# Gate and up weights of an expert as one 2 MB transfer, in a two-layer decoder trunk with 64 experts

## The chip, the cores and the metric

The kernel runs on one core of one Trainium2 chip. The metric is the device time of one execution in microseconds. The changed kernel is timed against the kernel before it on the same chip.

## What is computed

The reference is a decoder trunk of two layers on 256 tokens of width 1024, all in float32. Each layer runs an attention mixer beside a cross-attention into memory tokens, one output projection and a LayerNorm, then a mixture of experts and a second LayerNorm. The part that matters here is the mixture:

```python
def moe_ffn(x, w_router, router_bias, w_gate, w_up, w_down, ws_gate, ws_up, ws_down):
    ...
    gates = jnp.take_along_axis(aff, eidx, axis=-1)
    gates = gates / jnp.sum(gates, axis=-1, keepdims=True) * ROUTED_SCALE
    ...
    def expert_block(args):
        rows, e = args
        xb = x_pad[rows]
        h = jax.nn.silu(xb @ w_gate[e]) * (xb @ w_up[e])
        return h @ w_down[e]
    ...
    routed = jax.ops.segment_sum(yb * row_g[:, None].astype(yb.dtype), row_t, num_segments=n + 1)[:n]
    shared = (jax.nn.silu(xt @ ws_gate) * (xt @ ws_up)) @ ws_down
    return (routed + shared).reshape(B, S, D)
```

There are 64 experts with hidden width 256. Each token goes to 8 of them. `w_gate[e]` and `w_up[e]` are 1024 x 256 and `w_down[e]` is 256 x 1024, so each of the three matrices is 1 MB, and each layer has 192 MB of them.

## The kernel before

Each layer has an attention part and an expert part. The expert part goes through all 64 experts in 32 pairs; this text numbers the pairs of a layer 0 to 31. For each pair TensorE does a **gate pass** (32 matmuls, line 1219), an **up pass** (32 matmuls, line 1238) and a **down pass** (32 matmuls, line 1272). The down pass of a pair comes after the up pass of the next one, so the order on TensorE is gate 1, up 1, down 0, gate 2, up 2, down 1, and so on (function `unit`, line 1317). Between an up pass and the next down pass stand the scatter of an older pair's result (line 1280) and two small transposes (line 1191 and 1245), and in every fourth pair also the gather of the next eight experts' tokens (line 772). At the very end the order is gate 31, scatter, down 30, up 31.

The weights pass through a **ring** of four slots in on-chip memory, one expert (3 MB) in each, so two pairs have room. A slot has three parts of 1 MB: gate, up and down. SyncE (SP in the profile) issues all these transfers, in the order of its program. Each transfer is one instruction on SP at line 433, in `expert`. It moves 128 rows of 8 KB, one to each partition. All three parts are reloaded apart: `reload_gate` (line 455) waits until the gate pass that read the part is done and issues two gate transfers; `reload_up` (line 464) waits until the up pass is done and issues two up transfers; `reload_down` (line 435) waits for the down pass and issues two down transfers. The part of pair j is refilled with the weights of pair j+2. `reload` (line 473) is the first two of these in a row:

```python
reload_gate(l, units, i, b, kept)
reload_up(l, units, i, b, kept)
```

TensorE's gate pass waits for both gate transfers of its pair (semaphores `gate_landed`), its up pass for both up transfers (`up_landed`), its down pass for both down transfers (`down_landed`).

Some pairs are loaded in other ways. Pairs 0 and 1 come in during the attention part, each part apart. Pair 2 has its own lines ahead of the loops (reload_gate at line 578, one expert's up at 580), because one of its up matrices was loaded earlier. Pair 16 is the kept pair: its gate and up matrices, and in layer 0 one down matrix and in layer 1 both, are loaded long before into buffers that are free (`keep`, line 498), so 3 or 4 MB more room is there in the middle of the layer, and the ring need not bring them. Pair 31 is loaded by separate calls at the end of the layer (lines 608 to 610), and its down matrices in halves of 512 KB with rows of 2 KB (`last_down`, line 444). A branch for further rounds (line 614) is not entered with these inputs.

Of the kernel before, what the change touches and what calls it, by code (L numbers as in the profile page):

```python
# [16 lines left out]
P = 128  # L17
# [4 lines left out]
DEPTH = 2  # L22
# [4 lines left out]
NE = 64  # L27
# [48 lines left out]
def build_trunk(nc, x_in, mem_in, w_in_a, sinks, w_in_b, lambda_qk, subln_g, w_mem_kv, w_out, ln_g, ln_b,  # L76
                w_router, router_bias, w_gate, w_up, w_down, ws_gate, ws_up, ws_down, out):
    slopes = [alibi_slopes(MIX_HEADS), alibi_slopes(DIFF_HEADS)]
# [65 lines left out]
    with ExitStack() as ctx:  # L144
# [156 lines left out]
        def expert_loads(s, g, u, dn):  # L301
            n = KT * HID
            return [(s[:, 0:n].rearrange("p (k n) -> p k n", k=KT), by_row_run(g)),
                    (s[:, n:2 * n].rearrange("p (k n) -> p k n", k=KT), by_row_run(u)),
                    (s[:, 2 * n:3 * n].rearrange("p (f n) -> p f n", f=FT), by_row_pair(dn))]
# [102 lines left out]
        def _(sp):  # L408
# [18 lines left out]
            def expert(l, i, k, part):  # L427

                slot = (expert_slot0[l] + k) % RING
                e = RING * i + k  # L430
                srcs = [w[l, bass.ds(e, 1)].rearrange("a r n -> (a r) n") for w in (w_gate, w_up, w_down)]
                dst, src = expert_loads(ring[:, slot, :], *srcs)[part]
                sp.dma_start(dst, src).then_inc(sem(("gate_landed", "up_landed", "down_landed")[part] + f"{k}_{l}"), 16)
# [39 lines left out]
            def reload(l, units, i, b, kept=False):  # L473

                reload_gate(l, units, i, b, kept)
                reload_up(l, units, i, b, kept)

# [17 lines left out]
            def load_up_apart(l):  # L495
                sp.dma_start(up_apart, by_row_run(w_up[l, 0])).then_inc(sem(f"up_apart_{l}"), 16)

            def keep(l, part, e):

                w = (w_gate, w_up, w_down)[part][l, 2 * RES_PAIR + e]  # L500
                sp.dma_start(resident_view(part, e), by_row_pair(w) if part == 2 else by_row_run(w)).then_inc(sem(f"kept_{part}{e}_{l}"), 16)

# [1505 lines left out]
_INS = ["x", "mem", "w_in_a", "sinks", "w_in_b", "lambda_qk", "subln_g", "w_mem_kv", "w_out", "ln_g", "ln_b", "w_router",  # L2008
        "router_bias", "w_gate", "w_up", "w_down", "w_shared_gate", "w_shared_up", "w_shared_down"]

# [15 lines left out]
```

## Time and profile before

| what | value |
|---|---|
| median of 3 runs | 1208.66 us |
| lowest, highest | 1208.44 us, 1208.84 us |
| span of the profiled execution, first to last instruction | 1205.3 us |
| own time of the profiled execution | not given; the median is 3.4 us above its span |
| TensorE busy | 1158.6 us (96%) |
| VectorE, ScalarE, GpSimd busy | 347.2, 301.5, 54.9 us |
| bytes moved, mean rate | 446.93 MB, 371 GB/s |
| packets of SP's queue | 72208 |
| mean granted TensorE clock | 0.996 |
| first gate pass, last up pass, layer 0 | 140.4 us, 576.9 us |
| first gate pass, last up pass, layer 1 | 747.2 us, 1181.8 us |

All times in views of the trace are counted from the first instruction. A transfer is shown by the time at which SP issued it; when it had landed is shown as the time from issue to landing, for a group of transfers as minimum, median and maximum. A view of the chain of work shows, in order of time, the pieces that the end of the program followed from; a piece of DMA in it begins at the issue and ends at the landing.

### The profile page before, as it was taken

What the parts mean: (1) busy time and instruction counts of PE and PEld (TensorE: products, weight loads), DVE (VectorE), ACT (ScalarE), POOL (GpSimd) and SP (SyncE); (2) the same over time, 40 slices, a digit from 0 to 9 for tenths busy, and PEclk for the clock granted to TensorE, in tenths of its full rate; (3) what the DMA queues carried; (4) which work ended last, traced back from release to release, by engine and by line L of the source; (5) the groups of instructions that cost most, each with busy time, mean ns of one, the idle gap of its engine ahead of it and who ended that gap; (6) DMA issues with size and microseconds to landing.
All of it is one profiled execution on the core that took longest, in us unless ns stands there. A gap on an engine that the chain in (4) does not pass through costs nothing.

```text
span 1205.3 us, 22675 instructions
## 1 busy us (share of the span) xinstructions
PE 1158.6 (96%) x8948; PEld 708.5 (59%) x8948; DVE 347.2 (29%) x904; ACT 301.5 (25%) x713; POOL 54.9 (5%) x90
## 2 busy tenths in 40 slices
PE   9999999999999999998999999999999899999985
PEld 6875755555555555554687648555555555555552
DVE  1435512222122212221514456221222222222214
ACT  1453312222121212121213433122221212122212
POOL 1341000000001000000011000000000010000000
PEclk9999999999999999999999999999999999999998
DMA  9944899999999999999990568999999999999995
GB/s 362 364 175 145 310 411 420 422 421 422 422 421 420 410 421 420 422 421 421 387 360 20 205 244 332 411 418 421 422 422 422 422 415 399 409 421 422 421 420 209
DMA packets 74504, 446.93 MB, mean 371 GB/s; under 512 B 6977, under 2 KB 12481, under 8 KB 24897
## 3 DMA queue, kind: packets, MB, share of 16 engines
q1 hardware_dynamic: 72208, 441.22, 89.6%
q10 hardware_dynamic: 2224, 4.72, 1.0%
q8 instruction: 50, 0.82, 0.3%
q14 instruction: 22, 0.17, 0.0%
HBM read 444.86 MB, written 1.05 MB: 370 GB/s over the span
## 4 chain that ended last, share of the span: by engine, by line
PE 76%; DMA 19%; DVE 3%; issue 1%; ACT 1%; SPq 0%; DVEq 0%; ACTq 0%
DMA ring<-in_w_up 19%; PE bank L1238 16%; PE bank L1219 14%; PE bank L1272 13%; PE bank L791 7%; PE bank L772 7%; PE bank L1280 4%; PE bank L830 4%; PE bank L1245 1%; PE bank L1095 1%; PE bank L806 1%; PE bank L1118 1%; PE bank L994 1%; PE bank L1005 1%; DMA ring<-in_w_in_a 1%
## 5 line engine op out<-in xcount | busy, mean ns | idle before, releaser
L1238 PE MATMUL bank<-ring,work 128*64 128x256 f32 x1952 | 225.4, 380 | 13.7 <-DMA ring<-in_w_up 13.7
L1219 PE MATMUL bank<-ring,work 128*64 128x256 f32 x1984 | 227.8, 382 | 8.9 <-DMA ring<-in_w_gate 8.7
L1272 PE MATMUL bank<-ring,work 128*32 128x512 f32 x1904 | 222.0, 595 | 0.2
L1219 PEld LDWEIGHTS bank<-ring,work 128*64 128x64 f32 x1984 | 141.3, 137 | 116.9 <-issue 58.1
L1238 PEld LDWEIGHTS bank<-ring,work 128*64 128x64 f32 x1952 | 147.5, 137 | 81.6 <-issue 20.7
L1942 DVE SCALAR_TENSOR_TENSOR yhalf<-bank,gcol,yhalf 128x512 fp32r<-128x512 f32 x124 | 93.1, 751 | 214.6 <-ACT yhalf L1565 214.6
L1934 DVE TENSOR_TENSOR work<-work,bank 128x256 f32<-128x256 f32 x64 | 27.0, 421 | 367.0 <-PE bank L1238 367.0
L1565 ACT ACTIVATE yhalf<-bank,gcol 128x512 fp32r<-128x512 f32 x124 | 85.2, 687 | 181.4 <-PE bank L1272 181.4
L1272 PEld LDWEIGHTS bank<-ring,work 128*32 128x32 f32 x1904 | 57.4, 109 | 116.9 <-issue 109.9
L1402 ACT ACTIVATE work<-bank 128x512 f32<-128x512 f32 (+4 forms) x177 | 77.9, 440 | 95.1 <-PE bank L772 46.6
L1402 ACT ACTIVATE back<-bank 128x128 fp32r<-128x128 bf16 x64 | 17.7, 277 | 280.2 <-PE bank L1191 280.2
L791 PE MATMUL bank<-xT,ring 128*128 128x256 f32 x352 | 77.7, 379 | 0.0
L772 PE MATMUL bank<-hot,xhalf 128*128 128x256 f32 x512 | 72.8, 293 | 4.7 <-DVE work L1646 4.3
L1280 PE MATMUL bank<-yhalf,back 64*128 64x512 f32 x504 | 75.6, 418 | 0.0
L1555 ACT ACTIVATE work<-bank 128x256 f32<-128x256 f32 x64 | 24.6, 384 | 196.5 <-PE bank L1219 196.5
L1646 DVE COPY work<-bank 128x512 f32<-128x512 f32 (+3 forms) x77 | 51.3, 671 | 74.4 <-PE bank L772 57.7
L791 PEld LDWEIGHTS bank<-xT,ring 128*128 128x128 f32 x352 | 66.2, 190 | 9.0 <-issue 0.3
L772 PEld LDWEIGHTS bank<-hot,xhalf 128*128 128x128 f32 x512 | 64.9, 190 | 10.7 <-DVE work L1646 7.2
L1280 PEld LDWEIGHTS bank<-yhalf,back 64*128 64x128 f32 x504 | 42.4, 184 | 30.1 <-issue 23.9
L830 PE MATMUL bank<-ring,work 128*128 128x512 f32 x128 | 57.8, 594 | 0.0
L830 PEld LDWEIGHTS bank<-ring,work 128*128 128x128 f32 x128 | 23.2, 190 | 23.4 <-issue 23.1
L743 POOL TENSOR_TENSOR x<-xhalf 128x1024 f32<-128x1024 f32 x4 | 9.5, 2411 | 514.5 <-PE bank L1272 514.5
(190 smaller groups left out, 837.0 us busy)
## 6 DMA issues: line engine op xcount, KB each, us to landing
ring<-in_w_gate SPq DMA_DIRECT2D x124, 1024.0 KB, 13.8
ring<-in_w_up SPq DMA_DIRECT2D x122, 1024.0 KB, 15.7
ring<-in_w_down SPq DMA_DIRECT2D x119, 1024.0 KB, 14.7
ring<-in_w_in_b SPq DMA_DIRECT2D x3, 3072.0 KB, 18.5
ring<-in_w_out SPq DMA_DIRECT2D x4, 2048.0 KB, 13.8
home<-in_w_gate SPq DMA_DIRECT2D x4, 1024.0 KB, 18.0
ring<-in_w_down SPq DMA_DIRECT2D x8, 512.0 KB, 13.6
ring<-in_w_in_a ACTq DMA_DIRECT2D x1, 3072.0 KB, 19.5
```

The costliest lines, as they stand in the source:

```text
L772: last = pe.matmul(dst, a, b, start=(n == 0), stop=(n == len(pairs) - 1))
L791: mm = pe.matmul(bank_at(g)[:, c * 256:(c + 1) * 256], w[:, k, c0 + c * P:c0 + (c + 1) * P], moving[:, k, :], start=(k == 0), stop=(k == K ...
L830: last = pe.matmul(bank_at(g)[:], mixT[:, c, t * P:(t + 1) * P], item_view((l, f"out{half}"), 512)[:, c, :], start=start, stop=(done == KT))
L1219: last = pe.matmul(gate_bank[slots_of(e), 0:HID], xg[:, k, slots_of(2 * j + e)], w[e][:, k, :], start=(k == 0), stop=(k == KT - 1))
L1238: last = pe.matmul(up_bank[slots_of(e), 0:HID], xg[:, k, slots_of(2 * j + e)], w[e][:, k, :], start=(k == 0), stop=(k == KT - 1))
L1272: last = pe.matmul(yb[half][rows_of(t, e), :], hT[b][:, f, slots_of(e, t)], w[e][:, f, half * 512:half * 512 + 512], start=(f == 0), stop= ...
L1280: pe.matmul(sums[2 * t + half][:], back[b][rows_of(t), :], yhalf[rows_of(t), n, half * 512:half * 512 + 512], start=False, stop=False)
L1402: return act.activation(dst, src, ACT.Copy)
L1565: act.activation(yhalf[:, 0, half * 512:half * 512 + 512], yb[half][:], ACT.Copy, scale=gcol[:, j:j + 1])\
L1646: return dve.tensor_copy(dst, src)
L1934: dve.tensor_tensor(hidrow, sg, up_bank[:, 0:HID], ALU.mult).then_inc(s_("h_ready"), 1)
L1942: dve.scalar_tensor_tensor(out=yhalf[:, 1, part], in0=yb[half][:], scalar=gcol[:, j:j + 1], in1=yhalf[:, 0, part].bitcast(F32), op0=ALU.mu ...
```

## The change

The gate and up matrices of an expert are laid side by side on the host into one input, `w_gate_up`, of shape (layer, expert, 128, 2, 2048): for each expert and partition 8 KB of gate and then 8 KB of up, 16 KB in one run. In a slot of the ring the gate part and the up part lie next to each other, too. `reload` for a pair that isn't kept now waits for the up pass alone, and issues per expert one transfer of 2 MB, 128 rows of 16 KB, for both parts. It signals on `gate_landed`; `up_landed` is raised by SP when it issues the transfer, so the up pass no longer waits for a transfer of its own. Transfers that are still apart (pairs 0, 1, 2 and 31, the kept ones and the one beside them) read 8 KB runs out of the new input. The calls of `reload`, `reload_gate`, `reload_up` and `reload_down` stand where they stood. TensorE's program is the same.

```diff
@@ def expert(l, i, k, part):
                 e = RING * i + k
-                srcs = [w[l, bass.ds(e, 1)].rearrange("a r n -> (a r) n") for w in (w_gate, w_up, w_down)]
-                dst, src = expert_loads(ring[:, slot, :], *srcs)[part]
+                n = KT * HID
+                if part == 2:
+                    src = by_row_pair(w_down[l, bass.ds(e, 1)].rearrange("a r n -> (a r) n"))
+                    dst = expert_view(slot)[1]
+                else:
+                    src = w_gate_up[l, bass.ds(e, 1), :, part, :].rearrange("a p n -> (a p) n")
+                    dst = ring[:, slot, part * n:(part + 1) * n]
                 sp.dma_start(dst, src).then_inc(sem(("gate_landed", "up_landed", "down_landed")[part] + f"{k}_{l}"), 16)
@@ def reload(l, units, i, b, kept=False):
-                reload_gate(l, units, i, b, kept)
-                reload_up(l, units, i, b, kept)
+                if kept:
+                    reload_gate(l, units, i, b, kept)
+                    reload_up(l, units, i, b, kept)
+                    return
+                sp.wait_ge(sem(f"hidden_{l}"), units)
+                for k in (2 * b, 2 * b + 1):
+                    slot = (expert_slot0[l] + k) % RING
+                    sp.sem_inc(sem(f"up_landed{k}_{l}"), 16)
+                    src = w_gate_up[l, bass.ds(RING * i + k, 1)].rearrange("a p j n -> (a p) (j n)")
+                    sp.dma_start(ring[:, slot, 0:2 * KT * HID], src).then_inc(sem(f"gate_landed{k}_{l}"), 16)
@@ def load_up_apart(l):
-                sp.dma_start(up_apart, by_row_run(w_up[l, 0])).then_inc(sem(f"up_apart_{l}"), 16)
+                sp.dma_start(up_apart, w_gate_up[l, 0, :, 1, :].rearrange("p (k n) -> p k n", k=KT)).then_inc(sem(f"up_apart_{l}"), 16)
@@ def kernel(**inputs):
+    gate_up = [np.asarray(inputs[name]).reshape(DEPTH, NE, P, KT * HID) for name in ("w_gate", "w_up")]
     for name in _INS:
-        a = np.ascontiguousarray(inputs[name])
+        a = np.stack(gate_up, axis=3) if name == "w_gate_up" else np.ascontiguousarray(inputs[name])
```

The order of SP's transfers moves in two places of which the prediction speaks. The first is the start of the expert part of layer 0, where pair 3 is loaded after pair 1's passes. SP's program there before (`gated_0`, `hidden_0` and `down_done_0` count the passes done):

```order
L433 DMA ring<-in_w_gate 128x2048 [waits gated_0]
L433 DMA ring<-in_w_gate 128x2048
L433 DMA ring<-in_w_up 128x2048 [waits hidden_0]
L433 DMA ring<-in_w_up 128x2048
L433 DMA ring<-in_w_down 128x2048 [waits down_done_0]
L433 DMA ring<-in_w_down 128x2048
```

The same place in the changed kernel:

```order
L489 DMA ring<-in_w_gate_up 128x4096 [waits hidden_0]
L489 DMA ring<-in_w_gate_up 128x4096
L438 DMA ring<-in_w_down 128x2048 [waits down_done_0]
L438 DMA ring<-in_w_down 128x2048
L489 DMA ring<-in_w_gate_up 128x4096 [waits hidden_0]
```

The two gate transfers have gone from behind the gate pass to behind the up pass, and have become one with the up transfers. The second place is the body of the loop, one pair of it. Before, on SP (the ISA rows compute addresses):

```order
L433 ISA [waits gated_0]
L433 DMA ring<-in_w_gate 128x2048
L433 ISA
L433 DMA ring<-in_w_gate 128x2048
L433 DMA ring<-in_w_up 128x2048 [waits hidden_0]
L433 DMA ring<-in_w_up 128x2048
L437 REGISTER_ALU
L433 ISA [waits down_done_0]
L433 DMA ring<-in_w_down 128x2048
```

The same pair in the changed kernel:

```order
L489 ISA [waits hidden_0]
L489 DMA ring<-in_w_gate_up 128x4096
L489 ISA
L489 DMA ring<-in_w_gate_up 128x4096
L442 REGISTER_ALU
L438 ISA [waits down_done_0]
L438 DMA ring<-in_w_down 128x2048
```

In every pair the wait for the gate pass is gone, and what stood behind it stands behind the up pass.

## Rows read from the trace of the kernel before

**Rows 1.** The page, section 2: GB/s moved, 40 equal slices of the span.

```profile
GB/s 362 364 175 145 310 411 420 422 421 422 422 421 420 410 421 420 422 421 421 387 360 20 205 244 332 411 418 421 422 422 422 422 415 399 409 421 422 421 420 209
```

**Rows 2.** The page, section 4: chain that ended last, share of the span by engine.

```profile
PE 76%; DMA 19%; DVE 3%; issue 1%; ACT 1%; SPq 0%; DVEq 0%; ACTq 0%
```

**Rows 3.** Waits of TensorE: waiter, releaser, us in total, times, longest.

```profile
PE bank L1238 <- DMA ring<-in_w_up: 13.7, 13, 1.9
PE bank L1219 <- DMA ring<-in_w_gate: 8.7, 8, 1.1
```

**Rows 4.** Chain of work in order of time: start us, us, what.

```profile
317.08 25.56 DMA ring<-in_w_up
...
551.78 24.98 DMA ring<-in_w_up
...
923.88 25.55 DMA ring<-in_w_up
...
1157.22 24.42 DMA ring<-in_w_up
```

**Rows 5.** Timeline of TensorE, two stretches: start us, us, engine, line, operation, count.

```profile
160.27 3.67 PE L1219 MATMUL bank<-ring,work 128*64 128x256 f32 x32
163.77 0.60 PE L1238 MATMUL bank<-ring,work 128*64 128x256 f32 x4
...
300.04 3.62 PE L1238 MATMUL bank<-ring,work 128*64 128x256 f32 x32
...
305.20 3.64 PE L1272 MATMUL bank<-ring,work 128*32 128x512 f32 x32
308.77 3.67 PE L1219 MATMUL bank<-ring,work 128*64 128x256 f32 x32
```

**Rows 6.** Line 433 over the whole program: us from issue to landing.

```profile
DMA to landing us min/median/max: 4.9/14.9/25.6
```

**Rows 7.** Layer 0, pair 3's up transfers: SP's timeline, issue to landing.

```profile
155.71 0.80 SPq L433 DMA_DIRECT2D ring<-in_w_up  x2
...
DMA to landing us min/median/max: 6.7/7.7/8.8
```

**Rows 8.** Layer 0, pair 22 (its up transfers): SP's timeline, issue to landing.

```profile
417.08 0.81 SPq L433 DMA_DIRECT2D ring<-in_w_down  x2
420.82 0.86 SPq L433 DMA_DIRECT2D ring<-in_w_gate  x2
424.12 0.84 SPq L433 DMA_DIRECT2D ring<-in_w_up  x2
...
DMA to landing us min/median/max: 9.7/10.8/11.8
```

**Rows 9.** Layer 1, pair 3's up transfers: SP's timeline, issue to landing.

```profile
762.50 0.80 SPq L433 DMA_DIRECT2D ring<-in_w_up  x2
...
DMA to landing us min/median/max: 7.5/8.5/9.6
```

**Rows 10.** Layer 1, pair 22's up transfers: SP's timeline, issue to landing.

```profile
1030.94 0.81 SPq L433 DMA_DIRECT2D ring<-in_w_up  x2
...
DMA to landing us min/median/max: 7.9/9.5/11.1
```

**Rows 11.** Two transfers in a row, the second 2 MB, rows of 16 KB: issues, landings.

```profile
10.44 0.67 SPq L414 DMA_DIRECT2D ring<-in_w_in_a  x1
11.15 3.66 SPq L414 DMA_DIRECT2D ring<-in_w_mem_kv  x1
...
DMA to landing us min/median/max: 14.1/14.1/14.1
...
DMA to landing us min/median/max: 18.3/18.3/18.3
```

**Rows 12.** The four halves of layer 0's last down, rows of 2 KB.

```profile
L452 SPq DMA_DIRECT2D ring<-in_w_down x4: 597/610/612, 565.4 to 567.3; - x4
...
DMA to landing us min/median/max: 12.8/13.8/14.9
```

**Rows 13.** Two windows: us, busy time of engines, granted clock, DMA share, GB/s.

```profile
23.20:27.20 4.00, 4.00 (x20) 3.54 (x19) 0.32 (x1) 0.00 (x0) 0.00 (x0) 1.00 1.03 438
250.00:290.00 40.00, 40.00 (x352) 22.49 (x351) 8.64 (x23) 8.51 (x18) 0.00 (x0) 1.00 1.01 422
```

More of the change, by code:

```diff
@@ L76, in build_trunk @@
 def build_trunk(nc, x_in, mem_in, w_in_a, sinks, w_in_b, lambda_qk, subln_g, w_mem_kv, w_out, ln_g, ln_b,
-                w_router, router_bias, w_gate, w_up, w_down, ws_gate, ws_up, ws_down, out):
+                w_router, router_bias, w_gate_up, w_down, ws_gate, ws_up, ws_down, out):
     slopes = [alibi_slopes(MIX_HEADS), alibi_slopes(DIFF_HEADS)]
@@ L495, in load_up_apart @@
             def load_up_apart(l):
-                sp.dma_start(up_apart, by_row_run(w_up[l, 0])).then_inc(sem(f"up_apart_{l}"), 16)
+                sp.dma_start(up_apart, w_gate_up[l, 0, :, 1, :].rearrange("p (k n) -> p k n", k=KT)).then_inc(sem(f"up_apart_{l}"), 16)
             def keep(l, part, e):
-                w = (w_gate, w_up, w_down)[part][l, 2 * RES_PAIR + e]
-                sp.dma_start(resident_view(part, e), by_row_pair(w) if part == 2 else by_row_run(w)).then_inc(sem(f"kept_{part}{e}_{l}"), 16)
+                e_no = 2 * RES_PAIR + e
+                w = by_row_pair(w_down[l, e_no]) if part == 2 else w_gate_up[l, e_no, :, part, :].rearrange("p (k n) -> p k n", k=KT)
+                sp.dma_start(resident_view(part, e), w).then_inc(sem(f"kept_{part}{e}_{l}"), 16)
             rows = [[(biasrow[:], router_bias.rearrange("(o a) b -> o a b", o=1).broadcast_to([P, DEPTH, NE])),
@@ L2008 @@
 _INS = ["x", "mem", "w_in_a", "sinks", "w_in_b", "lambda_qk", "subln_g", "w_mem_kv", "w_out", "ln_g", "ln_b", "w_router",
-        "router_bias", "w_gate", "w_up", "w_down", "w_shared_gate", "w_shared_up", "w_shared_down"]
+        "router_bias", "w_gate_up", "w_down", "w_shared_gate", "w_shared_up", "w_shared_down"]
 def kernel(**inputs):
```

## Prediction

> **What bounds the kernel now.** I read the page first. TensorE is busy 96% of the span, but the chain that ended last gives DMA 19% [rows 2], and the slices of GB/s stand at 420 to 422 through most of both expert parts [rows 1]. So both are near their limit at once, and what decides is which of them the other waits for, stretch by stretch. The waits of TensorE name it: 13.7 us for up transfers and 8.7 us for gate transfers [rows 3]. These few waits tell how the layer ends. At 422 GB/s [rows 13], 1 MB (1.049 million bytes) takes 2.49 us, so a pair of experts, 6 MB, takes 14.9 us, while TensorE needs 3.5 + 5.2 + 3.6 = 12.3 us for it [rows 5], and a gather in every fourth pair. TensorE therefore gains on the loads until it has used up its lead. The chain in order of time shows where: it goes through up transfers that land at 317.08 + 25.56 = 342.64 us (pair 15) and at 551.78 + 24.98 = 576.76 us (pair 31) in layer 0, and at 949.43 and 1181.64 us in layer 1 [rows 4]. After 342.64 the kept pair 16 gives TensorE three passes with nothing to wait for, which puts the loads ahead again. The last up pass of each layer starts the moment its transfer lands, so the end of a layer is the end of a stream of transfers. Two things lengthen that stream: slower bytes, and time in which the queue is empty.
>
> How full the queue is, issue to landing tells. With an empty queue 1 MB lands 4.9 us after its issue [rows 6], which is 2.49 us of data and 2.4 us of start. While TensorE waits for loads, a transfer lands about 25 us after its issue: ten are queued. But at the start of a layer and again after the kept pair (pair 22), it is 7 to 12 us [rows 7 to 10], hardly more than what was issued with it. There the queue lives on each transfer coming as early as it does.
>
> **The change, part by part.** 54 pairs of transfers per layer (27 pairs of experts: 3 to 15 and 17 to 30) become 54 transfers with rows of 16 KB.
>
> *Rate.* The trace has one transfer of that form, w_mem_kv of layer 0. Its predecessor landed at 10.44 + 14.1 = 24.5 us, it at 11.15 + 18.3 = 29.4: 4.9 us for 2 MB, to about 0.1 [rows 11], against 4.97 for two of 1 MB. A second way: the four halves with rows of 2 KB ended at 567.3 + 14.9 = 582.2, after the up transfer's landing at 576.76 [rows 12, 4], so 1 MB took 2.72 us instead of 2.49. Each of the 16 DMA engines moved 32 rows for it instead of 8, so a row costs some 9 ns besides its bytes. Rows of 16 KB save each engine 8 rows per expert, 0.08 us. I take 4.89 us for 2 MB, 0.08 saved per expert. The bounds are 4.97 (nothing saved) and 4.79 (the window in which mostly that transfer moved shows 438 GB/s [rows 13], though its edges are rough).
>
> [...]
>
> *Start of the layer.* Gate transfers of pair 3 were issued after pair 1's gate pass, 3.5 us ahead of the up transfers; now both come at 155.71 [rows 7]. The first of them landed at 155.7 + 6.7 = 162.4; three transfers of 2.49 us back, at 154.9, the first gate transfer's data began, so what stood before it was in, and nothing is left in the queue at 155.71. The new ones land at 155.71 + 2.4 + 2 x 4.89 = 167.9, where pair 3's last up transfer landed at 156.1 + 8.8 = 164.9: **+3.0 us**. In layer 1: 762.50 + 2.4 + 9.8 = 774.7 against 762.9 + 9.6 = 772.5 [rows 9]: **+2.2**. From there the queue is full; pairs 4 to 15 are 24 transfers, **-1.9** in each layer.
>
> *The gate pass waits for up, too.* When TensorE is back at waiting, at pair 15, its gate pass now needs what the up pass needed. It starts when the up pass used to start, and the up pass starts a gate pass later, 163.77 - 160.27 = 3.5 us [rows 5]. The wait of the up pass is gone; it costs nothing more. So TensorE leaves pair 15 behind by 3.0 - 1.9 + 3.5 = **4.6 us** in layer 0 and 2.2 - 1.9 + 3.5 = **3.8** in layer 1. The kept pair follows, with TensorE never waiting, so this is carried whole to pair 20's up pass.
>
> *The queue dries again.* Pair 22's transfers are issued after that pass: 424.12 + 4.6 + 2.4 + 9.8 = 440.9, against 424.5 + 11.8 = 436.3 [rows 8], **+4.6** for the stream. (The down transfers before them, issued at 417.08 + 4.6, have landed by 429.1, and the new data begin at 431.1: the 2 us between are empty.) Layer 1: 1030.94 + 3.8 + 2.4 + 9.8 = 1046.9 against 1031.4 + 11.1 = 1042.5. That last landing came 3.7 us after the one before it (1030.9 + 7.9 = 1038.8), 1.2 more than the data take; I let that hitch come back: **+5.6** [rows 10]. Pairs 23 to 30 then save 16 x 0.08 = **-1.3**. The streams end at +3.3 and +4.3.
>
> *The last passes.* Pair 30's gate pass must wait for its up, too. From its landing to that of pair 31's last up transfer are 8 MB, 19.9 us. From its start to the start of up pass 31 TensorE needs two gate passes, one up pass with scatter and turns (305.20 - 300.04 = 5.2), two down passes (308.77 - 305.20 = 3.6 each) [rows 5], and a scatter of 1.3: 20.8. So TensorE is now late by itself at the very end: **+0.9** in each layer.
>
> SP issues fewer instructions, and its two semaphore raises per pair stand in waits of many us: nothing. Transfers that stay apart keep 8 KB rows; their new spacing in DRAM I price at nothing, covered by the attention parts for most, and at up to 1 us for pairs 2 and 31. Attention parts follow the layer's end as before.
>
> Sum: 3.3 + 0.9 + 4.3 + 0.9 = 9.4 us. The profiled execution would have a span of 1205.3 + 9.4 = 1214.7 us; on the median, 3.4 us above the span, 1208.66 + 9.4 = **1218.1 us**. A microsecond in the 2 MB transfer counts 2 + 24 + 2 + 16 = 44 times per layer, 88 in all, which makes it the term to watch.
>
> **The rivals.** *The queue never dries, and the rate wins (faster).* If 3.5 us of later issue were covered, all 108 transfers would save: -108 x 0.08 = -8.6, 1200.0 us. It decides from a backlog of 3.5 + 2.4 us at an up transfer's issue. In the stretches of waiting there are 20 us; but at pairs 3 and 22 [rows 7 to 10] the landings leave less than that. A 2 MB transfer of 4.79 us or less takes the same side: -8.8, 1209.3 us, no change. *No saving in rate.* At 4.97 us the sum grows by 88 x 0.08 = 7.0: 1225.1 us. For it speaks that the difference of 24.5 and 29.4 is read to a tenth; against it the line through 2 and 8 KB rows. *The phase shift costs nothing.* If the up pass's missing wait gave back the 3.5 us before pair 20 (another lead being used up), 7.0 us go and 1211.1 us remain; but between pairs 15 and 20 no transfer is waited for, and nothing there can give it back.
>
> **How the numbers follow.** The forecast, late issue and phase with some saving in rate, has 0.66; no saving in rate 0.13; the rate at 4.79 or the phase shift given back, about no change, 0.11; the rate winning outright 0.10. The range of 1209.0 to 1226.0 runs from the rate bound of 4.79 to that of 4.97 with a hitch more. A measurement of this kernel can tell about 0.2%, 2.4 us, from no change: faster 0.10, same 0.10, slower 0.80.
>
> **What would show it.** Right: GB/s above 425 where it was 422; new slices under 410 near 155, 430, 765 and 1035 us; TensorE's waits for up transfers gone but at pair 31, and those for gate transfers up to 2.5 us each; up pass 15 starting near 347.4, and up pass 31 near 576.90 + 4.2 = 581.1 and, with layer 0's 4.2 us, near 1191.2. Wrong: landings of pair 3 at or before 164.9, or 2 MB landings more than 4.95 or less than 4.8 us apart in the full queue.

## The result and the profile after

The changed kernel takes **1224.49 us** (median of 4 runs, 1223.32 to 1225.3), the kernel before it on the same chip 1208.55 us: ratio 1.0133, 95% interval 1.0119 to 1.0147, or 15.9 us slower. The forecast was 1218.1 us, in a range of 1209.0 to 1226.0. The direction is right and the time lies in the range, but the loss is 6.5 us larger than the 9.4 of the sum.

The profiled execution of the change took 1225.2 us with a span of 1223.5, so 1.7 us lie around the span. Against the span of before, 1205.3, that is +18.2. Every other run here has 1.7 to 1.9 us around its span, so the profiled execution of before was itself some 1.7 us faster than its median. Below, times of the whole kernel are medians, and positions inside it come from one profiled execution each.

The page of the change: busy time, GB/s and queues.

```profile
span 1223.5 us, 22633 instructions
...
PE 1170.9 (96%) x8946; PEld 727.4 (59%) x8948; DVE 347.1 (28%) x904; ACT 301.9 (25%) x713; POOL 54.9 (4%) x90
...
GB/s 362 353 172 167 309 367 423 426 427 427 426 378 403 402 396 424 426 425 422 372 360 10 227 231 345 366 424 423 427 426 427 414 360 401 393 425 426 425 422 170
...
q1 hardware_dynamic: 56656, 441.21, 88.0%
...
q8 instruction: 50, 0.82, 0.3%
```

The full stretches now stand at 425 to 427 GB/s where they stood at 420 to 422 [rows 1]. The faster bytes are real. But slice 6 (153 to 183 us) has 367 where it had 411, and slices 12 to 15 (336 to 459 us) have 378, 403, 402, 396 where they had 421, 420, 410, 421. Layer 1 shows the same: 366 for 411, and 414, 360, 401, 393 for 422, 415, 399, 409. The gain stands where the queue was full. The loss stands where it was short: at the start of the layer and from pair 15 to pair 22. A second thing is new: TensorE is busy for 12.3 us more (1170.9 for 1158.6), with the same program.

TensorE's waits for transfers in the change:

```profile
PE bank L1233 <- DMA ring<-in_w_gate_up: 29.2, 22, 2.5
```

The waits of the up pass are gone, and the gate pass has them all, up to 2.5 us each (line 1233 is the gate pass now, 1252 the up pass, 1286 the down pass, 489 the 2 MB transfer). In [rows 3] the two kinds together were 22.4 us in 21 waits of at most 1.9. There are about as many waits now, and they are longer.

Timeline of TensorE in the change: the gate passes of pairs 9, 10 and 11, and 15 and 30 of layer 0 (start us, us, idle time before and who ended it).

```profile
256.00 3.67 PE L1233 MATMUL bank<-ring,work 128*64 128x256 f32 x32 [0.49 <-DMA ring<-in_w_gate_up]
270.77 3.67 PE L1233 MATMUL bank<-ring,work 128*64 128x256 f32 x32 [2.46 <-DMA ring<-in_w_gate_up]
285.52 5.36 PE L1233 MATMUL bank<-ring,work 128*64 128x256 f32 x32 [2.45 <-DMA ring<-in_w_gate_up]
...
344.56 5.36 PE L1233 MATMUL bank<-ring,work 128*64 128x256 f32 x32 [2.45 <-DMA ring<-in_w_gate_up]
349.72 2.57 PE L1252 MATMUL bank<-ring,work 128*64 128x256 f32 x22
...
563.44 5.21 PE L1233 MATMUL bank<-ring,work 128*64 128x256 f32 x32 [2.42 <-DMA ring<-in_w_gate_up]
```

Two readings. Pairs 9, 10 and 11 follow each other in 14.77 and 14.75 us, the time of 6 MB, where [rows 13] made it 14.9. And some gate passes take 5.2 to 5.4 us instead of 3.67. There are eight of them in the program: pairs 11, 15, 26, 30 in layer 0 and 10, 14, 26, 30 in layer 1. They are eight times some 1.6 us, which is the extra busy time. What happened there, windows say (granted clock is the third number from the end, then DMA share and GB/s):

```profile
341.00:343.00 2.00, 1.10 (x12) 0.13 (x4) 0.86 (x2) 0.83 (x2) 0.00 (x0) 1.00 0.96 406
...
345.00:347.00 2.00, 2.00 (x13) 1.39 (x11) 0.00 (x0) 0.00 (x0) 0.00 (x0) 0.50 1.03 430
347.00:349.00 2.00, 2.00 (x16) 1.56 (x14) 0.00 (x0) 0.00 (x0) 0.00 (x0) 0.72 0.99 414
349.00:351.00 2.00, 2.00 (x22) 1.58 (x19) 0.00 (x0) 0.38 (x1) 0.00 (x0) 1.00 1.02 426
```

The granted clock fell to 0.50 as the gate pass began after its idle wait, and came back to 1.00 inside the pass: in windows of 0.5 us it is 0.73 from 344.5 to 345.0 us, 0.50 from 347.0 to 348.0, 0.86 from 348.0 to 348.5 and 1.00 behind that. The same wait ahead of pair 10 (2.46 us) was followed by a pass at full speed, so such a wait makes it possible and not certain. No slow pass in this kernel followed a wait of under 2.4 us.

### The profile page after: what moved, and what is told of

The parts are those of the page before. It is cut to its first block, busy times and chain, and to the rows that moved or that the text cites. A ratio compares the mean times of both kernels' runs of the same rounds, so it can differ in the third digit from the quotient of the medians.

```text
span 1223.5 us, 22633 instructions
## 1 busy us (share of the span) xinstructions
PE 1170.9 (96%) x8946; PEld 727.4 (59%) x8948; DVE 347.1 (28%) x904; ACT 301.9 (25%) x713; POOL 54.9 (4%) x90
## 3 DMA queue, kind: packets, MB, share of 16 engines
q1 hardware_dynamic: 56656, 441.21, 88.0%
## 4 chain that ended last, share of the span: by engine, by line
PE 71%; DMA 23%; DVE 3%; issue 1%; ACT 1%; SPq 1%; DVEq 0%; ACTq 0%
DMA ring<-in_w_gate_up 23%; PE bank L1233 15%; PE bank L1252 14%; PE bank L1286 10%; PE bank L805 7%; PE bank L786 7%; PE bank L844 4%; PE bank L1294 3%; PE bank L1109 1%; PE bank L820 1%; PE bank L1132 1%; PE bank L1008 1%; PE bank L1259 1%; PE bank L775 1%; PE bank L1019 1%
## 5 line engine op out<-in xcount | busy, mean ns | idle before, releaser
L1233 PE MATMUL bank<-ring,work 128*64 128x256 f32 x1984 | 241.0, 398 | 29.5 <-DMA ring<-in_w_gate_up 29.2
L1233 PEld LDWEIGHTS bank<-ring,work 128*64 128x64 f32 x1984 | 155.2, 143 | 137.8 <-issue 81.5
L1252 PE MATMUL bank<-ring,work 128*64 128x256 f32 x1952 | 225.4, 379 | 0.0
L1252 PEld LDWEIGHTS bank<-ring,work 128*64 128x64 f32 x1952 | 152.3, 137 | 60.5 <-issue 1.7
## 6 DMA issues: line engine op xcount, KB each, us to landing
ring<-in_w_out SPq DMA_DIRECT2D x4, 2048.0 KB, 13.3
```

What stands on the lines that cost most here:

```text
L1233: last = pe.matmul(gate_bank[slots_of(e), 0:HID], xg[:, k, slots_of(2 * j + e)], w[e][:, k, :], start=(k == 0), stop=(k == KT - 1))
L1252: last = pe.matmul(up_bank[slots_of(e), 0:HID], xg[:, k, slots_of(2 * j + e)], w[e][:, k, :], start=(k == 0), stop=(k == KT - 1))
```

## The experiments

All passes are compared by their start. Experiment 1, whose order of work is that of the kernel before, differs from it by up to 0.4 us in these columns, so smaller differences mean nothing. This table gives, for one profiled execution of each kernel, how much later than in the profile of before the up passes of pair 15 and pair 31 started. Layer 1's numbers are counted from its own first gate pass, so the delay of layer 0 is taken out. "Slow" is the number of gate passes over 5 us.

| kernel | L0 up 15 | L0 up 31 | L1 up 15 | L1 up 31 | slow | time against before, us |
|---|---|---|---|---|---|---|
| forecast | +4.6 | +4.2 | +3.8 | +5.2 | 0 | +9.4 |
| changed kernel | +6.9 | +8.6 | +5.2 | +9.5 | 8 | +15.9 |
| late issue alone | +3.2 | +3.8 | +3.3 | +5.9 | 0 | +10.1 |
| both waits alone | +6.4 | +7.0 | +3.3 | +4.1 | 3 | +10.0 |
| both waits, clock kept up | +3.6 | +3.2 | +3.5 | +4.9 | 0 | +7.5 |
| changed, rows of 8 KB | +8.7 | +9.9 | +8.6 | +11.6 | 6 | +20.4 |
| changed, clock kept up | +4.8 | +5.9 | +6.7 | +8.7 | 1 | +13.3 |
| 14 pairs merged | -0.9 | -2.9 | -1.1 | -1.7 | 4 | -5.2 |

**1. The layout alone.** All transfers are 1 MB, issued and waited for as before, out of the new input.

```diff
-                if kept:
+                if True:
                     reload_gate(l, units, i, b, kept)
```

> Only the layout of the input is new: gate and up side by side in DRAM, but every transfer is one of 1 MB with rows of 8 KB, issued and waited for as in the kernel before. Theory (late issue, the gate pass's wait for up, and a slowed TensorE clock carry the loss; the layout carries none): the time of the kernel before, 1208.6 us within 0.2%, 1 MB landing every 2.49 us in the full queue. Rival (reading 8 KB out of every 16 KB is slower): more than 2.49 us per MB and over 1212 us.

Measured: 1207.26 us against 1208.35, ratio 0.9991 (0.9981 to 1.0001). Laying gate and up side by side costs nothing. The price of nothing that the forecast gave it holds.

**2. Late issue alone.** 1 MB transfers with semaphores of their own; only the moment of issue is that of the change.

```diff
                 sp.wait_ge(sem(f"hidden_{l}"), units)
-                for k in (2 * b, 2 * b + 1):
-                    slot = (expert_slot0[l] + k) % RING
-                    sp.sem_inc(sem(f"up_landed{k}_{l}"), 16)
-                    ...
+                for part in range(2):
+                    for k in (2 * b, 2 * b + 1):
+                        expert(l, i, k, part)
```

> Transfers of 1 MB with semaphores of their own, so the gate pass waits for gate alone, but both are issued after the up pass. Theory: the queue runs dry at pairs 3 and 17 to 22, both layers, the end of the layers moves by 3.0 + 3 us and 2.2 + 3 us or so with nothing saved in rate: about +9, 1217 to 1218 us, no gate pass slowed to more than 4 us, since no wait is over 1.5 us. Rival (the late issue is covered, all the loss is the gate pass's wait and the clock): 1208.6 us.

Measured: 1218.43 us, ratio 1.0087 (1.007 to 1.0104), 10.1 us slower than before. Its waits and its granted clock:

```profile
PE bank L1250 <- DMA ring<-in_w_gate_up: 18.8, 18, 1.4
PE bank L1231 <- DMA ring<-in_w_gate_up: 12.2, 12, 1.2
...
die 0 (median of its cores): 1215.4 us, clock 0.997
```

30 waits, shared between the passes, none over 1.4 us, and no slow pass. The empty queue at the start of layer 0, as a window (DMA share and GB/s are the last two numbers):

```profile
153.00:157.00 4.00, 3.59 (x32) 2.00 (x32) 0.59 (x3) 0.62 (x2) 0.00 (x0) 1.00 0.22 45
```

The kernel before has 0.95 and 340 there. The late issue empties the queue and costs a good half of the loss, with TensorE at full clock. By pair 15 it costs 3.2 and 3.3 us in the two layers; the rest comes behind pair 16, 0.6 us in layer 0 and 2.6 in layer 1.

**3. Both waits alone.** 1 MB transfers issued as early as before; but the gate pass of pairs 3 to 15 and 17 to 30 waits for the up matrices, too.

```diff
                             pe.wait_ge(s_(f"kept_0{e}"), 16)
+                    if both:
+                        for e in range(2):
+                            pe.wait_ge(s_(f"up_landed{2 * b + e}"), rs * 16 + 16)
```

> Transfers of 1 MB issued when they were before, but the gate pass of pairs 3 to 15 and 17 to 30 also waits for the up transfers. Theory: waits of 2.5 us and more ahead of gate passes 10, 11, 14, 15, 26, 27, 30, and TensorE leaves pair 15 later by 3.5 us; +6 us from that, and half a dozen or more gate passes of 5.2 to 5.4 us instead of 3.7 add 3 to 5 us where they stand at pair 15 or 30: 1215 to 1220 us. Rival (the wait is only moved and costs nothing): 1208.6 us.

Measured: 1218.38 us, ratio 1.0085 (1.0063 to 1.0106), 10.0 us slower, as expected. Three gate passes were slow (pairs 15 and 30 of layer 0, pair 11 of layer 1), where half a dozen or more were expected. In its chain of work (start us, us, what) the wait for the up transfer, the slow gate pass of pair 15, and the up pass stand behind one another:

```profile
321.99 21.90 DMA ring<-in_w_gate_up
343.89 0.14 issue
344.02 5.36 PE bank L1236 x32
349.38 0.65 PE bank L1255 x6
```

Here no transfer has changed its place in SP's program, and still the up pass of pair 15 comes 6.4 us late: the gate pass's 3.5 us, 1.7 by which it was slow, and 1.2 by which its data came later (343.89 for 342.64). The 1.2 are not the joint wait's doing. Pair 9's second up transfer already landed at 254.4, for 253.2 before, and no gate pass had waited for up by then; pair 3's transfers, issued as before, had landed late in this execution. So the theory of a phase shift holds, and in layer 0 it was too cheap: the shift makes waits behind which TensorE's clock can fall (granted clock 0.50 from 345 to 347 us, inside the gate pass of pair 15, behind a wait of 2.63 us). In layer 1 pair 15 was at full speed, and its up pass is 3.3 us late.

The delay then empties the queue behind pair 15, since the next transfers are issued behind its passes:

```profile
361.00:364.00 3.00, 3.00 (x30) 1.28 (x24) 1.34 (x2) 1.35 (x2) 0.00 (x0) 1.00 0.45 115
```

The kernel before has 0.99 and 407 in this window, and experiment 2 shows no such hole. A DMA queue that runs dry is therefore no mark of late issue alone.

**4. The changed kernel with rows of 8 KB.** Gate and up lie one behind the other again; the transfer stays one of 2 MB, with two rows to a partition.

```diff
-                    src = w_gate_up[l, bass.ds(RING * i + k, 1)].rearrange("a p j n -> (a p) (j n)")
+                    src = w_gate_up[l, bass.ds(RING * i + k, 1)].rearrange("a j p n -> (a p) j n")
```

> The changed kernel, with its one transfer of 2 MB per expert at the same place and time, but gate and up of an expert are stored one behind the other, so that the transfer has two rows of 8 KB per partition. Theory (the saving is per row, 9 ns for each row of an engine): 2 MB take 4.97 us instead of 4.89 in the full queue, and the kernel is slower than the changed one by 88 x 0.08 = 7 us: 1231 us. Rival (the saving comes from fewer transfers, not longer rows): 4.89 us and 1224.5 us.

Measured: 1228.7 us, ratio 1.0167 (1.015 to 1.0184): 4.2 us above the changed kernel. Its window in the full queue, and the gate passes of pairs 9 to 11:

```profile
250.00:290.00 40.00, 35.61 (x302) 20.08 (x300) 7.58 (x19) 6.87 (x14) 0.00 (x0) 0.96 1.01 422
...
256.78 3.67 PE L1233 MATMUL bank<-ring,work 128*64 128x256 f32 x32 [0.67 <-DMA ring<-in_w_gate_up]
271.69 5.15 PE L1233 MATMUL bank<-ring,work 128*64 128x256 f32 x32 [2.60 <-DMA ring<-in_w_gate_up]
286.60 3.67 PE L1233 MATMUL bank<-ring,work 128*64 128x256 f32 x32 [1.13 <-DMA ring<-in_w_gate_up]
```

14.91 us for 6 MB, where the changed kernel has 14.76. The changed kernel's queue q1 has 56656 packets and this one's 70480 (pages), 128 more for each of the 108 merged transfers; over the sixteen DMA engines that the page counts, these are 8 rows for each transfer, 16 for a pair. The 0.15 us for 16 rows saved on each DMA engine make 9 ns a row. So the gain per transfer comes from the long rows and not from there being fewer transfers. The whole kernel was expected at 1231; its 4.2 us above the change are uncertain by some 2.7.

**5. Where the queue is short, split as before.** In the changed kernel the pairs 3 and 17 to 22 keep the early gate transfers of 1 MB, and their gate passes wait for gate alone. SP's loops over the pairs are divided for it (not shown); TensorE's program stays.

```diff
+SPLIT = {3, 17, 18, 19, 20, 21, 22}
...
-                if kept:
+                if kept or (isinstance(i, int) and UNROLL * i + b in SPLIT):
                     reload_gate(l, units, i, b, kept)
```

> The changed kernel, but pairs 3 and 17 to 22 are loaded as in the kernel before (four transfers of 1 MB, gate behind the gate pass); all others merged. Takes away the late issue where the queue is short. Theory: the queue stays full at the start and after the kept pair; what is left is the gate pass's wait for up (3.5 us at pair 15, 0.9 at 30), slowed gate passes, and less saving: 1210 to 1216 us, 9 to 14 below the changed kernel. Rival (the late issue costs little, the wait and the clock all): within 4 us of 1224.5.

Measured: 1214.51 us against 1207.94, ratio 1.0054 (1.0039 to 1.007). It is 10.0 us below the changed kernel, within the 9 to 14 expected. The up pass of pair 15 is still 5.7 us late in layer 0, with a slow gate pass ahead of it: the phase shift is left. (This is read from an execution that took 3.3 us more than the median.)

**6. Pairs 14, 15 and 30 split, too.** These are the pairs at which TensorE waits last before a stretch that decides.

```diff
+SPLIT = {3, 14, 15, 17, 18, 19, 20, 21, 22, 30}
```

> As e4_nodry, and also pairs 14, 15 and 30 loaded as before, so that 17 pairs per layer stay merged, all of them where the queue is full and TensorE has its lead. Theory: late issue, wait for up and slow clock cost nothing there, or are made good before the layer ends at a transfer; what is left is the rate, some 13 to 17 pairs x 2 x 0.08 per layer less what is lost on the way: 2 us per layer, about 1204.5 us (1203.5 to 1206.5). Rival (the rate's saving is eaten by a lead that TensorE loses at pairs 10 to 13): 1208.5 us or more.

Measured: 1207.45 us, ratio 0.9996 (0.9987 to 1.0005). The phase shift is gone (up 15 +1.2 and up 31 0.0 in layer 0), but it misses the expected 1204.5 (1203.5 to 1206.5). Pairs 4 to 6 are merged here, and their transfers came up to 2.0 us late; they are issued just behind the start, where the queue is still short.

**7. Pairs 4, 5 and 6 split, too.** Merged are now only pairs 7 to 13 and 23 to 29.

```diff
+SPLIT = {3, 4, 5, 6, 14, 15, 17, 18, 19, 20, 21, 22, 30}
```

> As e5_where, and also pairs 4, 5 and 6 loaded as before, since the queue is still short there (9.7 us from issue to landing at pair 6 in the changed kernel). Theory: three pairs fewer save 0.5 us less per layer, and an empty stretch of about 0.5 us at pair 6 goes: the time of e5_where within 1 us, 1203.5 to 1206.5 us. Rival (short queues at the start cost more than the count of empty time says): faster than e5_where by over 1.5 us.

Measured: **1202.78 us**, ratio 0.9959 (0.9945 to 0.9972), 5.2 us faster than before and 21.7 faster than the change. The theory had been within 1 us of experiment 6; it is 4.7 below, so the rival won, and merging pairs 4 to 6 had cost more than the count of empty time said. Half of the merged pairs were worth all of the gain:

```profile
PE bank L1245 <- DMA ring<-in_w_gate_up: 10.8, 7, 2.5
...
GB/s 361 367 176 139 308 413 420 425 427 427 422 422 421 409 423 425 427 425 420 388 365 16 209 241 333 411 419 425 426 426 424 422 418 396 414 424 425 427 419 202
```

425 to 427 in the middle of each stream, and no slice of the short stretches much under [rows 1]. 14 pairs with two saved times of 0.08 us, in two layers, are 4.5 us; 5.2 were measured. Four gate passes (11 and 27 in each layer) still run slow here. Behind them follow pairs whose waits take the delay up, so they cost nothing that can be seen.

**8. Keeping the clock up, first try.** The changed kernel with 8 matmuls on zeros ahead of the gate pass's wait in pairs 10, 11, 14, 15, 26, 27 and 30, for which TensorE's loops over the pairs were divided.

```diff
+                    if warm:
+                        for _ in range(warm):
+                            pe.matmul(gate_bank[:], zeros[:, 0:P], zeros[:], start=True, stop=True)
```

> The changed kernel with eight matmuls on zeros (1.8 us) ahead of the gate pass's wait in pairs 10, 11, 14, 15, 26, 27 and 30; their result is overwritten. Idle time of TensorE there falls from 2.5 us to under 1. Theory (the slow gate passes are TensorE's clock at half after an idle stretch): no gate pass over 4 us is left, mean granted clock above 0.99, and the slow passes at pairs 15 and 30 of layer 0 and 30 of layer 1 are worth 1.5 us each with what follows: 3 to 6 us below the changed kernel, 1219 to 1222 us. Rival (they are slow for another reason, such as reading weights while a transfer writes): gate passes of 5.2 to 5.4 us stay and the time is the changed kernel's or above.

Measured: 1227.33 us, ratio 1.0155 (1.014 to 1.0171): not faster but 2.8 us slower than the change, which is about the uncertainty, though one slow pass was left of eight and the clock was at 0.995. So the slow passes do follow from the clock that falls behind idle waits, and not from a transfer that writes while the weights are read. What they cost it does not tell. The page shows 66 instruction packets instead of 50. They go with the dividing of TensorE's loops: experiments 9, 10 and 11, with such matmuls and TensorE's loops whole, have 50, 51 and 51. Why a divided loop has more of them was not shown. In this kernel's trace the data of pair 11 and pair 30 of layer 0 landed some 1.3 and 1.5 us later than their bytes explain (286.70 and 567.00), each with an instruction packet begun about 3 us before, and TensorE waited 1.9 and 2.2 us there behind its zeros.

**9. Keeping the clock up in pair 30 alone.** 11 such matmuls, loops left whole.

```diff
-                        unit(r, OCTETS - 1, j, last=(j == OCT_PAIRS - 1))
+                        unit(r, OCTETS - 1, j, last=(j == OCT_PAIRS - 1), warm=WARMING if j == 2 else 0)
```

> The changed kernel with 11 matmuls on zeros (2.4 us) ahead of the gate pass's wait in pair 30 of each layer alone, in code that is no loop. Theory (an idle stretch of about 2.4 us lets TensorE's clock fall, and after gate pass 30 nothing makes the lost time good): gate pass 30 takes 3.7 us instead of 5.2, in both layers, and the last up pass comes 1.5 us earlier in each: 1221.5 us, 3 us below the changed kernel. Rival (the slow pass only fills time that would be waited later): 1224.5 us.

Measured: 1224.66 us, ratio 1.0131 (1.0115 to 1.0146), no gain. The gate pass of pair 30 is at full speed:

```profile
563.61 2.32 PE L1222 MATMUL bank<-zeros 128*128 128x512 bf16 x10 [0.16 <-issue]
565.86 3.67 PE L1236 MATMUL bank<-ring,work 128*64 128x256 f32 x32
```

But it starts 2.4 us later than in the change (565.86 for 563.44), for two reasons. Its data landed at 564.52, 1.2 us later than in the change, and the zeros held TensorE 1.2 us longer than the wait would have. So they took back most of the 1.5 to 1.7 us that a pass at full clock gives. (Of the 11 matmuls the trace holds 10.) Slow passes had moved to pairs 11, 15 and 27 in layer 0 and to 10, 15 and 27 in layer 1, and pair 15 of layer 1 was now slow, which it was not before. Where the clock falls is not fixed, so one spot can't be judged alone.

**10. Both waits alone, with the clock kept up.** Experiment 3 with 11 matmuls on zeros in pairs 7, 11, 15, 23, 27 and 30, which the loops can take without being divided.

```diff
-                            unit(r, o, j)
+                            unit(r, o, j, warm=WARMING if j == 3 else 0)
```

> e3_both with the same 11 matmuls on zeros ahead of the gate pass's wait in pairs 7, 11, 15, 23, 27 and 30 (loop bodies as they are). Theory: its slow gate passes at 15 and 30 of layer 0 go, 1.7 + 1.7 us or so of the 10.0 us that e3_both lost, and nothing else of weight moves: 1215 us. What stays, 6.5 us, is the later start of TensorE behind the up transfers. Rival (clock worth nothing here): 1218.4 us or, with the added work, above.

Measured: 1215.97 us, ratio 1.007 (1.0056 to 1.0084): 2.4 us less than without them, no slow pass, and the up pass of pair 15 late by 3.6 and 3.5 us. This is the 3.5 of the forecast, clean. The 2.4 us are not clear of the noise (the intervals overlap), and they are a balance: layer 0 ends 3.8 us earlier than in experiment 3, of which 1.2 were late data there, and layer 1 ends 0.8 us later.

**11. The changed kernel with the clock kept up in the same way.** The edit is that of experiment 10.

> The changed kernel with 11 matmuls on zeros (2.3 us) on TensorE ahead of the gate pass's wait in pairs 7, 11, 15, 23, 27 and 30 of each layer, at the places where the kernel with both waits took them without more code fetches than before. It asks what the slow passes cost the changed kernel itself. Theory (slow gate passes at 15 and 30 lie on the path): pairs 15 and 30 have no idle time over 0.3 us ahead of their gate passes, these take 3.67 us, the granted clock is at 0.99 or more, and the time is 3 to 6 us below the changed kernel's: 1218.5 to 1221.5, ratio near 1.010. Rival (the slow passes are covered; short queues and hitches set the time): passes at full clock, but 1223.5 to 1226, ratio 1.0125 or more. If slow passes only move to pairs 14 and 29, the clock stays near 0.987 and nothing is told apart.

Measured: 1222.44 us against 1209.1, ratio 1.012 (1.0104 to 1.0137). That is 2.1 us below the change by the medians, 2.6 by the differences to before; one such comparison is uncertain by 2 to 3 us. Timeline of pair 15 in layer 0, and a window (granted clock third from the end):

```profile
341.79 2.32 PE L1222 MATMUL bank<-zeros 128*128 128x512 bf16 x10 [0.16 <-issue]
344.08 3.67 PE L1236 MATMUL bank<-ring,work 128*64 128x256 f32 x32
...
344.00:350.00 6.00, 6.00 (x57) 4.79 (x58) 0.00 (x0) 0.38 (x1) 0.00 (x0) 1.00 1.01 422
```

In layer 0 the up pass of pair 15 is 4.8 us late, where the forecast had 4.6. The time lies between what the two theories gave (1218.5 to 1221.5, and 1223.5 or more). What the zeros give back is some 2 us, not 3 to 6, and hardly clear of the noise. What the fallen clock costs may be more, for the zeros cost time, too: at pairs 7 and 23, where TensorE did not wait, they made it some 2.5 us later, and the up pass of pair 15 in layer 1 is 6.7 us late for the change's 5.2. One slow pass was left in layer 1 (pair 14), and there the zeros came on top of it.

## Why the prediction was right, and what its sum missed

**The rate, per transfer: right.** 2 MB were taken at 4.89 us and 0.08 saved per expert. The pair of 14.76 us for 14.91 (experiment 4) is 0.075 saved per expert, and the changed kernel's first transfers in a stretch of waiting landed as far apart:

```profile
L489 SPq DMA_DIRECT2D ring<-in_w_gate_up x2: 328/330/333, 233.9 to 234.4; - x2
...
DMA to landing us min/median/max: 17.1/19.3/21.4
```

233.9 + 17.1 and 234.4 + 21.4 are 4.8 us apart, read to a tenth (4.89 in the trace). **On the whole kernel, smaller than taken:** 88 x 0.08 = 7.0 us were counted, 4.2 measured between experiment 4 and the change. With an uncertainty of two to three us the 7.0 are not excluded. Two things speak for them. In the traces the change has three slow gate passes at pairs 15 and 30, and experiment 4 only two, both at pair 15, which may make experiment 4 look up to 1.7 us better than it is. And experiment 7 gained 5.2 us with 56 merged transfers, where 0.08 each gives 4.5. No run settled it.

**Start of the layer: right, a little too small in layer 1.** Pair 3's transfers in the change:

```profile
L489 SPq DMA_DIRECT2D ring<-in_w_gate_up x2: 328/349/370, 155.9 to 156.3; - x2
...
DMA to landing us min/median/max: 7.6/10.4/13.3
```

They landed at 156.3 + 13.3 = 169.6, where 167.9 was forecast and 164.9 was before [rows 7]: +4.7 and not +3.0. The first came 7.6 us after its issue, 0.3 over 2.4 + 4.89; the second 6.2 us after the first, 1.3 over the data. But the kernel before is late in the same way, one transfer further on. The down transfers that follow, before and in the change:

```profile
L433 SPq DMA_DIRECT2D ring<-in_w_down x2: 328/380/433, 160.4 to 160.8; - x2
...
DMA to landing us min/median/max: 8.4/9.5/10.5
...
L438 SPq DMA_DIRECT2D ring<-in_w_down x2: 328/378/427, 160.5 to 160.9; - x2
...
DMA to landing us min/median/max: 11.6/12.7/13.7
```

They landed at 168.8 and 171.3 before, at 172.1 and 174.6 in the change: the stream is 3.3 us late, and the +3.0 was nearly right. The landing of pair 3 compared alone makes it look 1.4 us worse. In layer 1:

```profile
L489 SPq DMA_DIRECT2D ring<-in_w_gate_up x2: 328/333/338, 771.2 to 772.0; - x2
...
DMA to landing us min/median/max: 9.0/11.1/13.2
...
770.00:775.00 5.00, 4.59 (x42) 1.80 (x42) 0.77 (x4) 1.35 (x3) 0.00 (x0) 1.00 0.56 164
```

785.2, less the 8.6 by which the layer began later, is 776.6 for the 772.5 of [rows 9]: +4.1 and not +2.2, and the down transfers behind it have the same +4.1. The window shows the hole itself: DMA engines at 0.56, 164 GB/s. Experiment 2 is the clean test of this term, by the up pass of pair 15: +3.2 and +3.3 us at the old pace.

**The gate pass waits for up, too: right at full clock, and missing the clock.** The 3.5 us of the forecast are exact at full clock (experiment 10: 3.6 and 3.5). What failed is the clause "it costs nothing more". It overlooked what can follow a wait of 2.5 us in one piece, where there had been two shorter ones. The granted clock fell to 0.50, and in layer 0 the gate pass of pair 15, which stands on the path, took 1.7 us longer. At pairs 10, 11, 14 and 26 the next waits absorbed that; at pairs 15 and 30 there are none behind. With it goes the forecast of up pass 15: 349.7 us measured, 347.4 forecast, 1.7 by the slow pass and 0.6 by the stream.

**The queue dries again: right in place, too small.** Pair 22's transfers in the change, layer 0 and layer 1:

```profile
L489 SPq DMA_DIRECT2D ring<-in_w_gate_up x2: 333/604/876, 431.3 to 431.8; - x2
...
DMA to landing us min/median/max: 8.7/10.9/13.1
...
L489 SPq DMA_DIRECT2D ring<-in_w_gate_up x2: 332/332/332, 1045.0 to 1045.6; - x2
...
DMA to landing us min/median/max: 9.7/11.9/14.0
```

431.8 + 13.1 = 444.9 is 8.6 after the 436.3 of [rows 8], where +4.6 was forecast; 6.9 of it are TensorE's delay at pair 15, and 1.7 are new. In layer 1, 1059.6 less 8.6 is 8.5 after [rows 10], where +5.6 was forecast: 5.2 of delay and 3.3 on top. What makes the "on top" in layer 0 are the down transfers issued just before (424.1 and 424.7). They landed at 431.1 and 435.2, the first 2.1 us later than 2.4 + 2.49 after its issue, the second 4.1 us after the first instead of 2.5. So from 431.4 on the queue was empty but for one late part, much as forecast (the window from 431.4 to 432.2 us has a DMA share of 0.00), and that part, one of sixteen, came in at 435.1 (see the last section). Pairs 17 to 21 were late as well, up to 2.0 us, though the forecast had only pair 22 there. That added next to nothing: TensorE waited for none of them, its delay of 6.9 us is the same from pair 16 to pair 25, and they were in by 426.7, when the data of the down transfers began.

**The last passes.** In the changed kernel's chain of work, TensorE's own passes stand at the end of both layers, with no transfer between gate pass 30 and up pass 31:

```profile
577.28 3.60 PE bank L1233 x32
582.01 3.57 PE bank L1286 x32
585.59 3.60 PE bank L1252 x32
...
1191.68 3.60 PE bank L1233 x32
1196.41 3.57 PE bank L1286 x32
1199.98 3.60 PE bank L1252 x32
```

That TensorE itself would be last there was forecast, and so was the size at full clock: in experiments 4, 5 and 11, where gate pass 30 takes 3.67 us, up pass 31 starts 0.7 to 0.8 us behind the last landing, for 0.1 before. In the change gate pass 30 was slow in both layers (5.21 us). Up pass 31 starts at 585.6 and 1200.0, forecast were 581.1 and 1191.2. In layer 0 TensorE was 2.3 us behind the last landing. In layer 1 it was only 0.8 behind (the last transfer landed at 1199.1), since a transfer on the way had landed 1.5 us late and hid the slow pass. That this looks like the forecast's +0.9 is luck.

**The sum over causes.** The forecast's terms fall under the same heads as the experiments. Late issue had 7.6 us (start, dry queue, hitch, with each transfer still at its old pace); both waits 8.8 (3.5 and 0.9 per layer); the rate -7.0; together 9.4. Measured: late issue +10.1 (experiment 2), both waits +10.0 (3), of which some 2 may be the clock (10), rate -4.2 (4); together 15.9, which is what the change shows. That the parts add up to the tenth is luck, since each is uncertain by 1.5 to 3 us. But no large cause is missing. By these medians the 6.5 us too few are 2.5 of late issue, 1.2 of waits and clock, and 2.8 of rate. How the 6.5 really divide is not shown to better than 2 us. The traces say where to look: the late issue cost more than forecast in layer 1 (5.9 us there, against 3.8 in layer 0), and three slow gate passes stand at pairs 15 and 30.

**The rivals.** *The queue never dries* (1200.0) is out, the landings of pairs 3 and 22 show the holes. *The rate at 4.79* is out by the 14.76 us of a pair, which leave (14.76 - 4.97) / 2 = 4.9 for 2 MB, and *the phase shift costs nothing* by experiments 3 and 10. *No saving in rate* gave 1225.1, nearly the time measured, and is wrong all the same: experiment 4, which really has no saving, takes 1228.7. The time alone would have confirmed the wrong rival.

## What to carry to other kernels

Joining two transfers into one, as here, makes the earlier of them wait for the buffer of the later, and the earlier user wait for the data of the later. Price both, and do it only where the queue holds more than the delay of issue: here 14 of 27 pairs, and they brought all the gain that there was. When small waits of TensorE are gathered into a longer one, look at the granted clock of the pass behind it (here 0.50 instead of 1.00 behind some waits of 2.1 us or more) and at whether anything later absorbs the delay.

## What was not expected of the hardware

- The granted clock falls from 1.00 to 0.50 after some idle waits of 2.1 to 2.6 us (2.13 at the least, in experiment 5) between passes at full clock, and a gate pass of 3.67 us becomes one of up to 5.36. Which of equal waits does it changes from kernel to kernel: in layer 0 of the change the pass of pair 10 took 3.67 us behind 2.46 us of waiting and that of pair 11 5.36 behind 2.45, and in experiment 4 pair 10 took 5.15 behind 2.60. The waits of before (up to 1.9 us) and of experiment 2 (up to 1.4) never did. In the windows of pair 15 of layer 0 of the change the granted clock is 0.50 or 1.00, and between them (0.73, 0.72, 0.86) only where a window lies over a change from one to the other.
- With few transfers in the queue, a transfer often lands 1 to 2 us later than its bytes and start explain, with all data the same, and in the landings looked at one part of sixteen is late. The trace has sixteen marks for the landing of each transfer, and the page counts sixteen DMA engines; that each mark is one engine's is inferred from that. For pair 3's second transfer fifteen marks stand at or before 168.31 us and the last at 169.61; in the kernel before, for the down transfer that follows, at 167.30 and 168.81; for the two down transfers ahead of pair 22 in the change, at 428.97 and 431.13, and at 431.43 and 435.10. The transfer behind pair 3's second keeps the gap (170.80 and 172.10). In the full queue the marks of one transfer are spread over 2 us (253.91 to 255.87 for pair 9's second), so one mark that is late by 1 to 2 us does not stand out. In the window of pair 3's second transfer, 165 to 171 us, lies one instruction packet:

```profile
DMA packets 273, 2.51 MB, mean 418 GB/s; under 512 B 31, under 2 KB 31, under 8 KB 31
...
q8 instruction: 1, 0.02, 1.0%
```

1.0% of 16 engines' 6 us is 1.0 us of one engine's time, close to the 1.3 us by which that transfer was late. The kernel before has four landings in its expert parts that are 1.0 us or more later than issue and bytes explain (168.8, 396.4, 770.0 and 1042.5 us), and each has an instruction packet begun 2.5 to 4.2 us before it. That these packets cause the lateness fits experiment 8, too (16 packets more), but no run varied them alone, so it is argued and not shown. They are not the only cause either: none lies between the issue at 424.1 and the landing at 431.1. The holes of over 2 us have another cause again: there SP's issue came after the queue had run empty. In the change nothing moved from 769.8 to 772.1 us (window, 0 GB/s), and pair 3's transfers were issued at 771.2; in experiment 2 nothing moved from 765.0 to 767.6 us, and SP issued at 766.7.
